# A norm factor applied where matrix products are read, and a bias added on another engine

## The reference

```python
# first block, spatial gating: per head a 128x128 mixing of positions, plus a bias per position
g = jnp.einsum('bnpec,eqp->bnqec', v, w_s) + b_s.T[:, :, None]
return u * g.reshape(B, L, D_GMLP)
# first block, end of the feed-forward layer and the final norm
x = x + (jax.nn.silu(gate) * val) @ ffn_w_down[i]
return rmsnorm(x, norm_final)
# second block: norm, then every projection from it
h = rms_norm(x, norm_g)
proj = h @ w_in
(aq, ak, av, az, br, bk, bv, bz, bwd, bad, cq, cz, ga, gb, gc) = jnp.split(proj, offsets, axis=-1)
```

## Time and profile before

| | |
|---|---|
| median of 3 runs | 2485.74 us (2481.35 to 2487.22) |
| the profiled execution | 2486.66 us, its span 2485.0 us |
| TensorE busy | 2413.7 us, 97% |
| VectorE busy | 1536.2 us, 62% |
| ScalarE busy | 1136.0 us, 46% |
| mean granted TensorE clock | 0.986 of full speed |

### The profile page before, as it was taken

One profiled execution on the slowest core, in us unless ns is written; L12 is line 12 of the kernel. 1 busy time (PEld: TensorE's weight loads), 2 busy tenths in 40 slices (PEclk: granted clock), 3 DMA queues, 4 the chain that ended last, 5 costly groups with the idle time before them and its releaser, 6 DMA issues.

```text
span 2485.0 us, 50887 instructions
## 1 busy us (share of the span) xinstructions
PE 2413.7 (97%) x19960; PEld 2373.9 (96%) x19960; DVE 1536.2 (62%) x2064; ACT 1136.0 (46%) x1463; POOL 12.8 (1%) x27
## 2 busy tenths in 40 slices
PE   6999999999999999996899999999999999999999
PEld 6898999999999999996899999999999999999999
DVE  6556577667546667567876666776576554544554
ACT  5343345555434555434444445544465443434443
POOL 0000000000000000000000000000000000000000
PEclk9999899999999999998999999999999999999999
DMA  6353365555555555553333333333355365555554
GB/s 233 134 187 118 125 189 186 186 187 188 191 187 187 186 187 189 189 188 122 114 120 117 108 112 122 113 121 118 137 164 165 115 204 177 188 178 176 187 189 160
DMA packets 110149, 400.43 MB, mean 161 GB/s; under 512 B 12394, under 2 KB 12421, under 8 KB 109904
## 3 DMA queue, kind: packets, MB, share of 16 engines
q1 hardware_dynamic: 108000, 391.00, 47.8%
q0 software_dynamic: 2032, 7.67, 0.9%
HBM read 396.52 MB, written 2.10 MB: 160 GB/s over the span
## 4 chain that ended last, share of the span: by engine, by line
PE 92%; DVE 5%; ACT 1%; issue 1%; DMA 0%; DVEq 0%; SPq 0%; ACTq 0%
PE bank L418 91%; ACT w_hi L918 1%; DVE w_lo L1345 1%; DVE scratch L1394 1%; PE bank L620 1%; DVE s_k L1394 0%; DMA x<-in_xT 0%; DVE h_lo L1391 0%; DVE cum L1391 0%; DVE ping L1391 0%; DVE s_t L1391 0%; DVE root L1433 0%; DVE acc L1391 0%; DVE s_t L1398 0%; DVE s_k L1391 0%
## 5 line engine op out<-in xcount | busy, mean ns | idle before, releaser
L1345 DVE TENSOR_TENSOR w_lo<-raw,w_hi 128x1024 fp32r<-128x1024 f32 x736 | 896.9, 1224 | 794.6 <-ACT w_hi L918 789.8
L918 ACT ACTIVATE w_hi<-raw 128x1024 fp32r<-128x1024 f32 x736 | 778.9, 1060 | 1092.1 <-PE bank L418 1070.2
L418 PE MATMUL bank<-h_hi,w_hi 128*128 128x256 f32 x4016 | 1150.4, 286 | 26.9 <-DVE w_lo L1345 8.4
L418 PE MATMUL bank<-h_lo,w_hi 128*128 128x256 f32 x4016 | 1127.2, 281 | 0.0
L418 PE MATMUL bank<-h_hi,w_lo 128*128 128x256 f32 x4016 | 1126.0, 280 | 0.0
L418 PEld LDWEIGHTS bank<-h_hi,w_hi 128*128 128x128 f32 x4016 | 761.7, 190 | 36.4 <-issue 14.5
L418 PEld LDWEIGHTS bank<-h_lo,w_hi 128*128 128x128 f32 x4016 | 762.0, 190 | 3.3 <-issue 2.2
L418 PEld LDWEIGHTS bank<-h_hi,w_lo 128*128 128x128 f32 x4016 | 761.1, 190 | 0.0
L418 PE MATMUL bank<-m_hi,w_hi 128*128 128x256 f32 x704 | 196.5, 279 | 0.0
L418 PE MATMUL bank<-m_lo,w_hi 128*128 128x256 f32 x704 | 196.5, 279 | 0.0
L418 PE MATMUL bank<-m_hi,w_lo 128*128 128x256 f32 x704 | 196.5, 279 | 0.0
(11 more groups left out here) (413 smaller groups left out, 2777.5 us busy)
## 6 DMA issues: line engine op xcount, KB each, us to landing
raw<-in_units SPq DMA_DIRECT2D x736, 512.0 KB, 4.2
x<-in_xT SPq DMA_DIRECT2D x4, 512.0 KB, 5.9
memx<-in_memT POOLq DMA_DIRECT2D x4, 512.0 KB, 7.7
out_y<-obuf SPq DMA_DIRECT2D x8, 256.0 KB, 4.3
bias_t<-in_bias POOLq DMA_DIRECT2D x8, 192.0 KB, 2.9
dft<-in_dft POOLq DMA_DIRECT2D x1, 1024.0 KB, 7.8
decay<-in_decay POOLq DMA_DIRECT2D x1, 768.0 KB, 5.9
con<-in_con SPq DMA_DIRECT2D x1, 546.0 KB, 8.0
```

The costliest lines, as they stand in the source:

```text
L418: return pe.matmul(out, lhsT, rhs, start=start, stop=stop, skip_group_check=True)
L918: return act.activation(out, in_, ACT.Copy, scale=scale)
L1345: dve.tensor_tensor(w_lo[slot][:, :, :], raw[slot][:, :, :], w_hi[slot][:, :, :].bitcast(F32), ALU.subtract).then_inc(split_done, 1)
```

## The change

The norm factor root3 is no longer applied to x. In the second half of the down projection, x times the weight gains is split into h_hi and h_lo at the end of each quarter (gained_pair, high_pair, low_pair), and VectorE multiplies by root3 whenever a bank of the second block's input projection is read: lx, pr, pk, pv, bz (k0), q and k (qk), az, avf, cqs, czs and the merge gates. Most of these reads were copies or activations of ScalarE, which now takes what VectorE has written. The lora group goes into another bank (2) and before the norm sums, which follow head unit 0; the lora products follow head units 3 to 5 in threes, and the prefix steps head units 6 to 11. The gate's bias is loaded into all partitions by a broadcast DMA and added by VectorE from the bank; its 12 matmuls are gone. Some buffers move. The diff without the buffer placement:

```diff
         pw = place("pw", [P, 4, P], 97 * K)
-        bs = place("bs", [1, HY * P], 99 * K)
+        bs = place("bs", [P, HY, P], 99 * K)
         prod = [place(f"prod{i}", [P, 384], (38 + 6) * K + 1536 * i) for i in range(4)]
...
         merged_ready = sem("merged_ready")
+        cross_gates = sem("cross_gates")
         stored = sem("stored")
...
             pool.wait_ge(free_early, 1)
-            for dst, src in ((ws[:, :, :], "ws"), (pw[:, :, :], "pw"), (bs[:, :], "bs")):
+            for dst, src in ((ws[:, :, :], "ws"), (pw[:, :, :], "pw")):
                 pool.dma_start(dst, a[src]).then_inc(mixer_in, 16)
+            pool.dma_start(bs[:, :, :].rearrange("p e q -> p (e q)"), a["bs"].broadcast_to([P, HY * P]))\
+                .then_inc(mixer_in, 16)
             pool.wait_ge(free_inv, 1)
...
                     o = banks[3 + e // 2][:, (e % 2) * T + c * P:(e % 2) * T + (c + 1) * P]
-                    mm(o, gvt[:, c, e * P:(e + 1) * P], ws[:, e, :], True, False)
-                    m = mm(o, con[0:1, CC["ones"][0]:CC["ones"][0] + P], bs[0:1, e * P:(e + 1) * P], False, True)
+                    m = mm(o, gvt[:, c, e * P:(e + 1) * P], ws[:, e, :])
                 if e % 2:
...
 
-            norm_sums(acc_x, acc_g)
-            group(1, h_hi, h_lo, tiles=1, arriving=True)
+            tiles_in = [n.next("dve") for _ in range(8)]
+            group(2, h_hi, h_lo, tiles=1, ready=(dve_for_pe, tiles_in[1::2]))
 
...
                 turned(2, v_).then_inc(psum_for_act, 1)
-                from_act()
+                pe.wait_ge(bank_read[1], n.now(("fill", 1)))
                 for c in range(2):
...
 
-            late_counts = {"dve": 16, "act": 21}
+            late_counts = {"dve": 16, "act": 20}
             pair_counts = {("fill", 0): 2, ("fill", 1): 2, "split": 16, "keys": 1, "sums": 1, "qk": 1}
...
                 heads(k)
-                if k == 1:
+                if k == 0:
+                    norm_sums(acc_x, acc_g)
+                if k == 3:
                     from_act()
                     pe.wait_ge(lora_in, 16)
-                if 1 <= k <= 4:
-                    for j in (2 * k - 2, 2 * k - 1):
+                if 3 <= k <= 5:
+                    for j in range(3 * k - 9, min(3 * k - 6, 8)):
                         if j >= 2:
...
                             .then_inc(psum_for_act, 1)
-                if k == 4:
+                if k == 5:
                     from_act(2)
...
                         n.next(("fill", b))
+                    if half:
+                        for s in range(2):
+                            high_pair(4 * q + 2 * s)
+            split4()
+            n.next(("fill", 2))
             act.activation(spare[:, 0:1], con_("eps6"), ACT.Sqrt)
...
             to_dve(act.activation(root3[:, :], root3[:, :], ACT.Sqrt, bias=con_("eps12"), scale=1.0 / D))
-            high_halves(scratch2, h_hi)
-
-            split4()
-            group_done()
-            n.next(("fill", 1))
-            copy(lx[:, 1:257], p2(1)[:, 0, :]).then_inc(bank_read[1], 1)
             from_dve()
...
                 if k % 4 == 3:
-                    group_done()
                     n.next(("fill", (k // 4) % 2))
-                if k == 3:
-                    copy(small["pr"][:, 1:257], p2(0)[:, 0, :])
-                    copy(small["pk"][:, 1:257], p2(0)[:, 1, :]).then_inc(bank_read[0], 1)
                 if k == 7:
-                    act.wait_ge(keys_ready, n.next("keys"))
-                    copy(small["pv"][:, 1:257], p2(1)[:, 0, :])
-                    to_dve(act.activation(small["k0"][:, :], p2(1)[:, 1, :], ACT.Tanh, scale=0.5))
+                    from_dve()
+                    to_dve(act.activation(small["en"][:, :], small["k0"][:, :], ACT.Tanh, scale=0.5))
                 if k == 9:
...
                 if k == 11:
-                    act.activation(qr[:, :, :], p2(0), ACT.Square).then_inc(qk_squared, 1)
-                    copy(qk[:, :, :], p2(0)).then_inc(bank_read[0], 1)
+                    act.wait_ge(bank_read[0], n.now(("fill", 0)))
+                    act.activation(qr[:, :, :], qk[:, :, :], ACT.Square).then_inc(qk_squared, 1)
                 if k == 12:
...
                 if k == 15:
-                    to_pe(copy(avf[:, :], p2(1)[:, 0, :]))
-                    to_dve(act.activation(az[:, :], p2(1)[:, 1, :], ACT.Tanh, scale=0.5))
+                    from_dve()
+                    to_dve(act.activation(small["en"][:, :], az[:, :], ACT.Tanh, scale=0.5))
 
...
                 if k % 4 == 3:
-                    h, b = k // 4, (k // 4) % 2
-                    group_done()
-                    n.next(("fill", b))
-                    copy(cqs[:, 2 * h:2 * h + 2, :], p2(b)).then_inc(bank_read[b], 1)
+                    n.next(("fill", (k // 4) % 2))
 
...
             ep4 = small["ep"][:, :].rearrange("p (c t) -> p c t", c=NCH)
-            pair_counts = land(16) | {"unit": 16, ("fill", 0): 2, ("fill", 1): 2, "keys": 1, "qk": 1}
+            pair_counts = land(16) | {"unit": 16, ("fill", 0): 2, ("fill", 1): 2, "qk": 1}
             for k in range(16):
...
                 heads(k, 0)
-                if 1 <= k <= 4:
-                    for j in (2 * k - 2, 2 * k - 1):
+                if 3 <= k <= 5:
+                    for j in range(3 * k - 9, min(3 * k - 6, 8)):
                         psum()
...
                                              bias=col("a0", j)))
-                if k == 4:
+                if k == 5:
                     to_dve(copy(spare[:, 1:2], icl[:, 0, 0:1]))
-            with n.loop(HEADS_A - 1, {"psum": 21, "dve": 3} | pair_counts) as i:
+            with n.loop(HEADS_A - 1, {"psum": 21, "dve": 5} | pair_counts) as i:
                 late(lambda k: heads(k, i + 1))
...
                     high_halves(scratch3, mh_hi, quarters=MEM_SPLIT[h])
-                group_done()
                 n.next(("fill", h % 2))
-                act.activation(czs[:, 2 * h:2 * h + 2, :], p2(h % 2), ACT.Silu).then_inc(bank_read[h % 2], 1)
+                act.wait_ge(bank_read[h % 2], n.now(("fill", h % 2)))
+                cz = czs[:, 2 * h:2 * h + 2, :]
+                act.activation(cz, cz, ACT.Silu).then_inc(cross_gates, 1)
 
...
                         split4()
-                        group_done()
-                        act.wait_ge(bank_read[1], n.now(("fill", 1)))
                         n.next(("fill", 0))
-                        act.activation(gate[:, :, :], p2(0), ACT.Tanh, scale=0.5).then_inc(bank_read[0], 1)
+                        act.wait_ge(bank_read[0], n.now(("fill", 0)))
+                        to_dve(act.activation(gate[:, :, :], gate[:, :, :], ACT.Tanh, scale=0.5))
                         split4(2)
...
                 s = 2 * (k % 2)
-                to_act(tt(y_part[:, s:s + 2, :], gu[:, 2 * k:2 * k + 2, :],
-                          banks[3 + k][:, :].rearrange("p (s t) -> p s t", s=2), ALU.mult))
+                for i in range(2):
+                    step(tt(y_part[:, s + i, :].rearrange("p (c q) -> p c q", c=2),
+                            banks[3 + k][:, i * T:(i + 1) * T].rearrange("p (c q) -> p c q", c=2),
+                            bcast(bs[:, 2 * k + i, :], 2), ALU.add))
+                settle()
+                to_act(tt(y_part[:, s:s + 2, :], y_part[:, s:s + 2, :], gu[:, 2 * k:2 * k + 2, :], ALU.mult))
                 settle_act()
...
                         read(tt(t, t, p2(b), ALU.add), b)
-                    for s, b in enumerate(pair):
-                        own_bank(b)
-                        if half:
+                    if half:
+                        for s, b in enumerate(pair):
+                            own_bank(b)
+                            gained_pair(4 * q + 2 * s, lambda t: gains[:, 1, bass.ds(t, 1)])
+                        for s in range(2):
+                            low_pair(4 * q + 2 * s)
+                        for s in range(2):
                             running(4 * q + 2 * s, q == 0 and s == 0, gained=True)
...
 
+            split4()
+            n.next(("fill", 2))
             from_act()
...
             inverted(root3)
-            normalised(x, lambda t: gains[:, 1, t:t + 1], scratch2, h_hi, h_lo, root3)
-            step(dve.reciprocal(root2[:, :], root2[:, :]))
-
-            split4()
-            n.next(("fill", 1))
-            own_bank(1)
+            read(tt(lx[:, 1:T + 1], p2(2)[:, 0, :], root3[:, :], ALU.mult), 2)
+            own_bank(2)
             step(tt(lt[:, :], lx[:, 0:T], lx[:, 1:T + 1], ALU.subtract))
...
             settle_act()
+            step(dve.reciprocal(root2[:, :], root2[:, :]))
             for t in ("pr", "pk", "pv"):
...
                     n.next(("fill", (k // 4) % 2))
+                    group_done()
+                if k == 3:
+                    step(tt(sm["pr"][:, 1:T + 1], p2(0)[:, 0, :], root3[:, :], ALU.mult))
+                    read(tt(sm["pk"][:, 1:T + 1], p2(0)[:, 1, :], root3[:, :], ALU.mult), 0)
```

(45 more changed lines are left out.)

## The result

The changed kernel takes **2504.58 us** (median of 7 runs, 2495.14 to 2506.50), the kernel before beside it 2485.3 (2481.35 to 2487.22). The ratio is 1.0069, 95% interval 1.0054 to 1.0083: slower by 0.7%, where I forecast 2481 and no change that can be told. The profiled execution's span is 2503.2 us against 2485.0.

The account below looks back on a forecast made before the run. TensorE, busy 97% of the span, was taken as the bound. The terms -13.2 + 1.3 - 6.7 + 12.6 + 1.2 = -4.8 took the median 2485.74 to 2481 us, 8-in-10 range 2469 to 2490.

Parts of the forecast that it names:

- Gate: Spatial gate stage: without the one-row bias matmuls the clock stays full, 15.8 us against 29.0, -13.2; VectorE's additions cost nothing.
- Rival 3: Gate stage: the clock still falls, from the position-mixing matmuls alone, costing 1.7 to 6.8 us; about 2485; chance 10%.
- Down quarters: Ends of the last down quarters: added splits of x delay VectorE's next low half; two quarters lose 0.65 each, +1.3.
- Transition: From the last down matmul into the first late stage: the norm factor no longer precedes the split; -6.7 together.
- The -1.9: First late stage, part of -6.7: the 2.60 gap and half clock behind it go, 76.32 becoming 74.38.
- Head loop: Seven turns: waits of 0.65 at the squares and 1.15 at the q/k operands, 1.8 a turn, +12.6.
- Cross attention: Cross attention: ScalarE waits for VectorE's bank read before each Silu, plus one later root; +1.2 (0 to 3).
- VectorE's bank reads: Bank reads moved to VectorE: 0.68 per 512 columns; the skill's surcharge of 0.065 us each was not added.
- Merge: Merge: a bank read and a tanh, 1.3, lie beside units four ahead of need; nothing, uncovered 24 x 1.3.
- Rivals 1: Head loop: the waits vanish as VectorE's issue overlaps more, a turn losing 0.65 or less; 2473; chance 20%.
- Rival 2: Head loop: VectorE's added work and the held high half all land on the path, 3.8 x 7 = 27; 2495; 10%.
- Rival 4: Transition misjudged: the wait at k=12 is shorter or its half clock absent, 2476, or longer, 2486; chance 14%.

Follow-up runs that it names:

- e1: The kernel before with the gate's part of the change alone (bias added by VectorE, 12 bias matmuls gone): 2482.90 us, ratio 0.9987.
- e2: The changed kernel with the gate's bias matmuls put back, so the norm factor's part alone: 2503.21 us, ratio 1.0068.
- e5: e3 with VectorE reading a full bank before the low half that stood ahead of it in the head stage: 2471.19 us, ratio 0.9932.
- e6: e3 with ScalarE's tanh of az moved behind the next unit's high half: 2476.28 us, ratio 0.9957.
- e4: The changed kernel once more, unchanged: 2500.30 us, ratio 1.0061.
- e3: The changed kernel with 12 one-column matmuls, product unread, added ahead of the merge loop: 2486.38 us, ratio 1.0010.
- e10: The changed kernel with 6 one-column matmuls, product unread, added ahead of the merge loop: 2475.38 us, ratio 0.9957.
- e11: The kernel before with 12 one-column matmuls, product unread, added ahead of its merge loop: 2486.53 us, ratio 1.0002.
- e16: The changed kernel with 9 one-column matmuls, product unread, added ahead of the merge loop: 2487.36 us, one run.

## Why the prediction was wrong

Term by term, forecast and measured:

- **Gate, -13.2: measured -13.4.** The granted clock stays at 1.00 from 257.36 to 277.00 here and through the gate stage of e1. In e2, with the bias matmuls back, the stage takes 29.06 at 0.77. So the one-row matmuls between the others were what let it fall, and VectorE's additions are covered. Rival 3 did not come. By the rule of the Trainium skill that I weighed there ("TensorE: Matmul & The Clock Gate", "Why this matters for your kernels", a matmul over few rows takes as long as one over 128) it would have been 2.9; the measurement decides against it.
- **Down quarters, +1.3: +1.8 to 2.2** (734.57 against 736.34 to 736.73 at the pace of 2.80). There are gaps of 0.51 and 0.63 at the two quarters named (forecast 0.65 each), and 0.6 to 1.0 more that I did not trace.
- **Transition, -6.7: -3.7** in this profile, -2.0 to -5.1 in the seven other runs of the norm part as it was made (T to the chunk products 89.38 to 92.40). The chain came as worked out: head unit 0 at T+12.1 (forecast 12.0), unit 6 at T+43.6 (42.4), the wait at unit 12 12.06 (11.6), squares at T+76.4 (74.7), chunk products at T+90.7 (89.5). The -1.9 that I added for the first late stage did not come: it takes 76.42, before 76.32. The gap of 2.60 and the half clock behind it are gone, but this stage has the turn's waits as well, 0.62 at the scores and 0.53 at the squares. I wrote that VectorE is 3 us ahead there; it is 1.4 ahead (its last operand is done at 1200.87, TensorE takes it at 1202.25).
- **Head loop, +12.6: +12.7.** The mechanism came as forecast. By starts a turn is 1.43 later at the scores (forecast 1.15, without the smaller waits ahead of them) and 0.70 more at the squares (0.65), 2.1 in all against 1.8, and e5 and e6 confirm both causes by taking them away. That the total agrees so well is in part luck. The loop has seven turns, and the first late stage is the first of them; so with this stage exempt, as I had it, six were left, 10.8. Measured are six turns of 2.1 and 0.1 in the first. Against my two terms for the row of seven turns, -1.9 and +12.6, it measured 2.0 more.
- **Cross attention, +1.2: +2.2.** The wait at the first memory unit is 1.75 where it was 0.66, and the last late stage has a wait of 0.69 at the scores, which I had not counted.
- **VectorE's bank reads** cost what the rows said. A read of 512 columns from a bank, then an operation of the same size with both sources in SBUF, from the timeline after:

```profile
1341.54 0.68 DVE L1386 TENSOR_TENSOR qk<-bank,root 128x512 f32<-128x512 f32 x1
```

```profile
1285.92 0.69 DVE L1386 TENSOR_TENSOR m_Q<-m_Nt,con 128x512 f32<-128x512 f32 x1
```

  The surcharge for a bank that the Trainium skill gives ("VectorE: DVE Perf Modes", "The TRN2 errata") does not appear: 0.68 against 0.69. With the bank reads still on VectorE and only their order changed (e5), the loop loses nothing.
- **Merge, 0: +11 to 13.** Here the prediction failed. The step is "nothing; uncovered it would be 24 x 1.3": it prices the new reads and tanhs, rightly at nothing, and stops there. What the twelve removed matmuls do to all that stands behind them in TensorE's list was no term of my sum. Taking them out moves the merge loop to a place where each turn waits for instructions twice. From the first memory unit to the end e4 takes 639.11, the kernel before 627.79 and e3, the same code with the loop back in its old place, 626.42. The step costs 11.3 against the one and 12.7 against the other; of that 7.8 are e4's three second gaps themselves. The rest I put down mainly to the clock, which over 10 us around the second restart is 0.66, 0.66 and 0.83 in e4; around e3's single restarts it is 1.00, 0.83 and 0.83. With the loop in its old place (e3) the change cannot be told from the kernel before: 1.0010 (0.9997 to 1.0022).

Corrected with these sizes: -4.8, and +11.5 (merge), +3.0 (transition with the first late stage), +1.0 (cross), +0.9 (quarters), -0.1 (gate and loop) give +11.5, or 2497. What is left of the 18.2 between the spans is the slower pace of this profile (6.0 over the projections, and 1.9 behind them, which I have as the remainder and did not measure), less 1.2 at the start. The medians lie between: 2500.30 in one set of runs, 2504.58 in another. Whether the changed kernel draws the slower pace more often than the one before stays open; a profile shows one execution.

Rivals 1 and 3 did not come. Rival 2, "VectorE paces the loop", has part of its mechanism (the high half held behind ScalarE's wait) confirmed at 2.1 a turn, below the 3.5 from which it would have decided alone. Rival 4, a misjudged transition, came as 3.0 us, by the first late stage and a little at each step and not by the wait at unit 12. That the result is slower came from none of my cases.

## What to carry to other kernels

Before costing an edit that removes or adds instructions, look whether a loop behind it shows gaps at its turns, and count the packets of the instruction queue. If a loop is loaded anew each turn, a few instructions more or less ahead of it can be worth as much as the edit, so compare two versions at a like place of that loop.

Where a hand-over is moved from one engine to another, the work is rarely the cost; what is already queued ahead of it on the new engine is, and putting the short read first can give all of it back.

And a lead of an engine in the stretch before a loop must be measured, not assumed, before the first turn is exempted from the loop's wait.

## What the runs showed of the hardware

- **Instruction loading.** In the kernel before and after, the merge loop's instructions are loaded in packets of some 16 KB, nine a turn. TensorE stands still for 2.2 to 2.8 us at each turn, as a packet comes. At place -12 a second gap of 2.0 to 3.2 us follows after two matmuls (e1) or three. With the loop 3 or 6 matmuls later nothing is loaded at its turns. The head loop has no instruction packets in its later turns (none from 1300 to 1700 us) and no such gap.
- **The clock behind such a gap.** The granted clock over 10 us around the first turn, in the kernel after (two gaps), in the kernel before (one) and in e10 (none):

```profile
2082.00:2092.00 10.00, 5.02 (x31) 4.62 (x31) 4.43 (x5) 2.59 (x3) 0.00 (x0) 0.74 0.47 158
```

```profile
2075.00:2085.00 10.00, 7.51 (x51) 7.32 (x50) 4.47 (x6) 2.77 (x4) 0.00 (x0) 0.83 0.45 154
```

```profile
2073.00:2083.00 10.00, 10.00 (x88) 10.00 (x88) 5.57 (x6) 3.85 (x5) 0.00 (x0) 1.00 0.52 166
```

  So a single gap can bring half clock too. It does so at all three turns of the kernel before, but at two of three in e3, e11 and e16, where the clock stays at 1.00 once. A gap's price is therefore not the same each time.
- **Two paces at one clock.** With the granted clock at 1.00 and no gap, 24 matmuls take 2.800 us in some stretches and 2.827 in others, 1% apart. Which stretch has which changes between executions of the same code (742.75 and 736.73 us to T). It may be what spreads the runs of one kernel over 5 us or more; that is not shown, and no run here tells what sets it.
- **Rows of a matmul and the clock.** Twelve fp32 matmuls over one row, each between matmuls over 128 rows, cost 13.4 us in all, though TensorE had no idle time. At full clock a pair takes 0.83 us, and a mixing matmul alone takes 0.22 in the kernel after (twelve from 257.36 to 260.04), so 12 x 0.61 = 7.3 go with them. The other 6.1 are the half clock from 263.4 on. Whether the single row costs this or the steady change between two kinds of matmul, no run tells apart.
